# Feed-forward stage of a hybrid decoder block: norm 2 of tokens 0 to 511 before the rest, with the first products between, and half of the low parts on VectorE

## The reference, cut to what matters

```python
x = x + merged @ w_out[l]
h2 = rms_norm(x, norm2_g[l])
x = x + (jax.nn.silu(h2 @ w_ffn_gate[l]) * (h2 @ w_ffn_up[l])) @ w_ffn_down[l]
```

## Time and profile before

| what | value |
|---|---|
| median of 3 runs | 2294.84 us (2293.65 to 2296.45) |
| the profiled execution, its own time | 2295.39 us |
| span in the profile, first to last instruction | 2293.4 us |
| PE busy | 2131.7 us, 93% |
| DVE, ACT, POOL busy | 1287.4, 757.0, 921.2 us |
| norm 2 begins (first transfer of its gain) | 1587.13 us |
| first product of the first chunk | 1625.60 us |
| last product of the first chunk ends, first down matmul | 1667.97 us |
| mean granted TensorE clock | 0.967 |

### The profile page before, as it was taken

How to read it: one execution, slowest core, us unless ns; L and a number is a source line. 1 busy time by engine, 2 the same in 40 slices (tenths; PEclk the granted TensorE clock), 3 DMA queues, 4 the chain that set the end, 5 groups by cost and what they waited for, 6 DMA issues and landing times. The chain is left out here.

```text
span 2293.4 us, 29780 instructions
## 1 busy us (share of the span) xinstructions
PE 2131.7 (93%) x10088; PEld 1724.4 (75%) x10088; DVE 1287.4 (56%) x1744; ACT 757.0 (33%) x1326; POOL 921.2 (40%) x733
## 2 busy tenths in 40 slices
PE   4999989998999999999999699997799999999999
PEld 3787777777877777777877478886688888888887
DVE  4557676852275675675676466557544444444444
ACT  3223232321154454454454420002422222223322
POOL 3322222222244344344344233332855555555552
PEclk7999999999899999999999799998799999999999
DMA  3211111222414314314324172221111111111111
GB/s 104 48 34 46 28 46 30 49 48 78 99 29 101 78 41 101 78 41 101 78 41 110 70 270 74 91 83 46 56 56 44 37 47 55 55 55 55 55 55 73
DMA packets 137775, 153.84 MB, mean 67 GB/s; under 512 B 7664, under 2 KB 112112, under 8 KB 137728
## 3 DMA queue, kind: packets, MB, share of 16 engines
q1 hardware_dynamic: 136000, 150.07, 23.8%
q10 hardware_dynamic: 1728, 3.15, 0.4%
HBM read 107.06 MB, written 20.97 MB: 56 GB/s over the span
## 5 line engine op out<-in xcount | busy, mean ns | idle before, releaser
L123 POOL TENSOR_TENSOR w_hi<-w_raw,w_ones 128x64 fp32r<-128x64 f32 x88 | 34.2, 389 | 763.7 <-PE gla_g L147 362.2
L478 POOL TENSOR_TENSOR sb_rows<-sb_beta,sb_rest 128x128 f32<-128x128 f32 (+7 forms) x128 | 166.1, 1302 | 250.8 <-DVE sb_rest L833 250.8
L833 DVE TENSOR_TENSOR_SCAN sb_rest<-sb_rest 128x128 f32<-128x128 f32 (+7 forms) x128 | 205.6, 1614 | 33.6 <-ACT sb_beta L684 33.6
L126 POOL TENSOR_TENSOR w_lo<-w_raw,w_hi 128x1024 fp32r<-128x1024 f32 x88 | 218.5, 2483 | 7.3
L839 DVE TENSOR_TENSOR sb_wt_lo<-sb_t,sb_wt_hi 128x512 fp32r<-128x512 f32 x192 | 106.4, 554 | 172.3 <-ACT sb_wt_hi L692 170.3
L692 ACT CAST sb_wt_hi<-sb_t 128x512 fp32r<-128x512 f32 x192 | 92.6, 482 | 234.0 <-PE sb_t L577 232.8
L147 PE MATMUL sb_g<-h_hi,w_hi 128*128 128x512 f32 x544 | 161.1, 421 | 3.7 <-DVEq L737 3.7
L147 PE MATMUL sb_g<-h_lo,w_hi 128*128 128x512 f32 x544 | 156.3, 413 | 0.0
L147 PE MATMUL sb_g<-h_hi,w_lo 128*128 128x512 f32 x544 | 153.1, 406 | 0.0
L147 PE MATMUL gla_g<-h_hi,w_hi 128*128 128x512 f32 x480 | 132.1, 408 | 1.8 <-DVEq L1251 1.8
L577 PE MATMUL sb_t<-ident,sb_rows 128*128 128x128 f32 x576 | 102.4, 289 | 32.1 <-DVE sb_wt_lo L839 32.0
(11 more groups left out here) (310 smaller groups left out, 5084.6 us busy)
## 6 DMA issues: line engine op xcount, KB each, us to landing
w_raw<-w_in SPq DMA_DIRECT2D x64, 512.0 KB, 8.1
ff_raw_g<-w_ffn_gate SPq DMA_DIRECT2D x11, 1024.0 KB, 5.4
ff_raw_u<-w_ffn_up SPq DMA_DIRECT2D x11, 1024.0 KB, 5.8
ff_raw_d<-w_ffn_down SPq DMA_DIRECT2D x11, 1024.0 KB, 4.9
sb_qs<-sb_q_st SPq DMA_DIRECT2D x32, 256.0 KB, 5.1
sb_kh<-sb_k_st SPq DMA_DIRECT2D x32, 256.0 KB, 5.1
sb_kl<-sb_k_st SPq DMA_DIRECT2D x32, 256.0 KB, 5.0
mp_sig<-gates_t SPq DMA_DIRECT2D x16, 512.0 KB, 4.4
```

Source lines behind the costliest of these rows:

```text
L123: self.nc.gpsimd.tensor_tensor(hi[:, 0:64], raw[:, 0:64], self.ones[:], ALU.mult)
L126: self.nc.gpsimd.tensor_tensor(lo, raw, hi, ALU.subtract).then_inc(self.ready, 1)
L478: nc.gpsimd.tensor_tensor(rows[tb // 4][:, tb % 4, 0:width], beta[:, n % 2, 0:width], rest[:, n % 2, 1:width + 1], ALU.mult).then_inc(row_ ...
L833: nc.vector.tensor_tensor_scan(back, back, back, 1.0, ALU.mult, ALU.bypass).then_inc(scanned, 1)
```

## The change

The transposes and high and low parts of tiles 0 to 3 (tokens 0 to 511) are done first, and they fill all eight banks. P1 g, P1 u, P2 g and P2 u of the first chunk then run one at a time, each followed by the transposes of one pair. A pair now needs its late tile (i+4) scaled into a new buffer `xg_late`, and transposes both tiles again into banks 2, 3, 6 and 7. `xg_late` has two places and lies where the weights' ring places 4 and 5 are, so these two are filled only after the last pair's transposes (`third_product`). VectorE takes over the low parts of P5 and P7 of each pair from GpSimd. In every chunk the third product is now P5 and the fourth P3. GpSimd's list of the first chunk is written out anew.

```diff
+    ORDER = (P1, P2, P5, P3, P6, P7, P4)
...
+                def first_gate_up(norm):
+                    low(0, G, P1, 1)
+                    sums_1(G, 0)
+                    low(1, U, P1, 2)
+                    for m in (G, U):
+                        low(2 + m, m, P2, 3 + m)
+                    norm(0)
+                    sums_1(U, 0)
+                    norm(1)
+                    norm(2)
+                    for m in (G, U):
+                        low(4 + m, m, P5, 5 + m)
+                    norm(3)
+                    for m in (G, U):
+                        sum_2(m, 0, 0)
+                    for m in (G, U):
+                        sum_4(m, 0, 0)
...
-                    for n, op in enumerate((P5, P7, P6, P4)):
+                    for n, op in ((2, P6), (3, P4)):
                         pool.wait_ge(t_high, 4 * pair + n + 1)
...
+                def third_product():
+                    act.wait_ge(pair_done, 4 * PP)
+                    for n in (4, 5):
+                        high(n, n, 0)
+
+                for pair in range(PP - 1):
+                    pair_high(pair)
+                pair_high(PP - 1, third_product)
...
+                    tt(h[P3][1][:, :, cols], b22, h[P3][0][:, :, cols], ALU.subtract).then_inc(b_low, 1)
+                    for n, (op, t) in enumerate(((P5, t1), (P7, t3))):
+                        dve.wait_ge(t_high, 4 * pair + n + 1)
+                        tt(h[op][1][:, :, cols], t, h[op][0][:, :, cols], ALU.subtract).then_inc(t_low_dve, 1)
...
+                for i in range(PP):
+                    first_low(i, 0)
+                scale(PP)
+                for i in range(PP):
+                    first_low(i, 1)
                 for pair in range(PP):
+                    combine(pair)
+                    if pair + 1 < PP:
+                        scale(PP + pair + 1)
...
+                def transposes(pair):
+                    pe.wait_ge(xg_ready, PP + pair + 1)
+                    pe.wait_ge(b_low, 2 * PP + pair)
+                    need(pe, t_made, 4 * pair)
+                    late = xg_late[:, pair % 2, :]
+                    for bank, src, k0 in ((2, late, 0), (3, xg[:, pair, :], 0), (6, late, KH), (7, xg[:, pair, :], KH)):
+                        flip(bank, src, k0).then_inc(pair_done, 1)
...
                             multiply(slot(2 * n + m), bank, p)
+                            if norm and p in (P1, P2):
+                                transposes(2 * n + m)
```

More of the change, by code:

```diff
@@ L1798, in gate_up @@
                                 sum_4(m, ch, at)
+                def first_gate_up(norm):
[15 more added lines that the diff above has]
+                        sum_4(m, 0, 0)
+                    for n, p in enumerate(ORDER):
+                        if n >= 3:
+                            for m in (G, U):
+                                low((2 * n + m) % RING, m, p, 2 * n + m + 1)
                 def down_low(ch):
@@ L1893, in gate_up @@
                             y_round(3, ch)
[L1895 to L1900, removed]
-                    high(n, n, 0)
+                for i in range(PP):
+                    first_high(i)
+                    if i == 2:
+                        high(0, 0, 0)
+                for n in range(1, 4):
+                    high(n, n, 0)
+                def third_product():
[5 more added lines that the diff above has]
+                pair_high(PP - 1, third_product)
                 gate_up(0, lambda n: n % RING)
@@ L1943, in low @@
[L1943 to L1951, removed]
+                    dve.wait_ge(b12_kept, pair + 1)
@@ L2044, in _, with flip @@
             def _(pe):
+                def flip(bank, src, k0):
+                    for q in range(KH):
+                        ins = nc.tensor.transpose(tr[bank][:, q, :], src[:, (k0 + q) * P:(k0 + q + 1) * P], c["ident"][:])
+                    return ins
                 def transposes(pair):
[L2046 to L2054, removed]
+                    pe.wait_ge(xg_ready, PP + pair + 1)
[4 more added lines that the diff above has]
+                        flip(bank, src, k0).then_inc(pair_done, 1)
                 def multiply(slot, bank, op):
@@ L2103, in down_block @@
                         ins.then_inc(d_done, 1)
-                for pair in range(PP):
-                    transposes(pair)
+                for i in range(PP):
+                    pe.wait_ge(xg_ready, i + 1)
+                    for half in range(2):
+                        flip(2 * i + half, xg[:, i, :], half * KH).then_inc(tr_done, 1)
                 gate_up(0, lambda n: n % RING, 0, norm=True)
```

117 lines of the change are left out of this document (61 added, 56 removed).

## The result

The changed kernel takes 2298.71 us (median of 14 runs, 2294.60 to 2302.52) against 2293.22 for the kernel before (14 runs, 2287.39 to 2297.09): a ratio of 1.0024, 95% interval [1.0014, 1.0034]. It is slower by about 5.5 us. The profiled execution took 2301.57 us, span 2299.7, which is 6.3 more than before's 2293.4.

The account below looks back on a forecast made before the run. TensorE, busy 93% of the span, bounds the kernel; the start and length of its last unbroken run of products decide. 2295.39 + 4.3 = 2299.7, or 2299.1 against the median; it said 2299.5, range 2292.5 to 2306.

Parts of the forecast that it names:

- Head: Norm 2's first 32 transposes: cost unchanged, 6.97 us; P1 g starts about 1601.2, gaining nothing; pair 0's transposes at 1604.7.
- Pairs: Loop over late tiles: pair 0 takes 10.4 us, later ones 9.2 to 10.45; pair 3's transposes start at 1633.5 to 1636.0.
- P5 g: First half-product of P5, now third product: could start at about 1639.4 to 1643.6, gaining 1.1 us or losing 3.
- P3 g: First half-product of the fourth product: waits 6.3 us for GpSimd's sums and weight low part, starts at 1648.6 to 1652.7.
- The unbroken run: TensorE's last products of the first chunk without a wait: 8 half-products, 21.8 us, ending at 1670.4 to 1674.5.
- The number: Whole kernel's time: +4.3 us gives 2299.7 for an execution like the profiled one, 2299.1 against the median; 2299.5 said.
- Other chunks: Chunks after the first, with P5 ahead of P3: TensorE has no gap to lose there, 0.
- no meeting: Rival: VectorE's new low parts meet no GpSimd operation; full-clock period 8.0, -3.6 us, 2291.5; chance 0.17.
- clock stays up: Rival: same order, TensorE's clock stays full in the loop, all pairs at 9.2 us; +1.9, 2297; chance 0.19.
- VectorE passed over: Rival: a low part on VectorE waits until GpSimd is idle, P5 starts at about 1653; +12, 2307.5; chance 0.12.

Follow-up runs that it names:

- e1_lows_gpsimd: The changed kernel with all four low parts of each pair back on GpSimd, none of these on VectorE; 2288.19 us, ratio to before 0.9976.
- e7_p5_low_first: The changed kernel with the next scaling ahead of VectorE's low parts and, in the last pair, P5's low part right behind T3; 2290.43 us, ratio 0.9992.
- e8_filled_p5: The changed kernel with the next scaling ahead of VectorE's low parts, plus 14 extra matmuls behind pair 3's transposes; 2290.84 us, ratio 0.9991.
- e9_first_filled: e7_p5_low_first with 8 extra matmuls behind pair 3's transposes, in the wait in front of P5 g; 2289.72 us, ratio to before 0.9986.

## Why the prediction was right

The direction, the place and the mechanism held. Step by step:

- *Head.* P1 g at 1600.32 (said 1601.2) and pair 0's transposes at 1603.79 (1604.7): 0.9 us sooner, since the 32 transposes took 5.62 us, not the 6.97 of the earlier trace rows; the clock had risen at 1596.9 where it rose at 1599.5 before. P1 g gained nothing by itself, as said.
- *Pairs.* Said 10.4, then 9.2 to 10.45 with a leaning to the upper end; measured 9.94, 10.25, 10.15. The two low parts were priced at 1.2 us of work and 1.7 of turns, 2.9 in all; the rows have 2.92, 2.94, 2.94 and 3.09. Pair 3 at 1634.13 lies in 1633.5 to 1636.0.
- *P5 g* at 1641.46 (1639.4 to 1643.6), and behind P5 the wait for GpSimd's weight low part, as said. GpSimd's last low part ended at 1644.22 (1642.3 to 1646.4).
- *P3 g* at 1650.57 (1648.1 to 1652.2), 0.4 behind the middle. From the end of the last low part it took 6.35 us; 6.3 was said.
- *The unbroken run.* This is the mis-sized term. Eight half-products were put at 21.8 us, all at full clock; they took 23.68 (1650.57 to 1674.25). About 1.6 of the 1.9 us more come from the clock, which fell to half for 3.5 us just behind the wait, and which the filled wait gave back; 0.3 from P3 g itself, which behind a wait takes 2.98 us also at full clock. The prediction had allowed for a low clock in P5, where it was hidden, and not in P3, where it is not; the kernel before, with a wait of 1.59 us there, gave no sign of it. With it, +6.3 in the trace in place of +4.3, which is also beyond the +1.9 to +6.0 of the sum. The forecast's own range, +2.9 to +6.5, holds it, but the prediction gives no working for that one.
- *The number.* 2299.5 was said and 2298.71 measured, and part of that nearness is luck. The sum set out from a median of 2294.84 for the kernel before, and in this measurement it has 2293.22. As a change, +4.7 was said and +5.5 measured.
- *Other chunks.* 0 was said: from the first down matmul to TensorE's end it took 622.32 us before and 622.30 after.

The rivals: *no meeting* fell by the 1.25 to 1.76 us of L1995; *clock stays up* by 0.50 at 1610.50. *VectorE passed over* did not happen to the new low parts, all eight took their turn. But it exists. In `e1_lows_gpsimd` it came back, on the same product as in the earlier trace rows:

```profile
1643.67 4.82 DVE L2002 TENSOR_TENSOR ff_u<-ff_u,ff_cg 128x512 f32<-128x512 f32 x1
```

In the kernel after, the same product at 1649.93 took 1.04 us with the same GpSimd operations in front of and behind it, and in the other nine kernels 1.04 to 1.73. The two in which it was passed over are the two in which GpSimd makes all four low parts of the last pair; whether that is the reason no run shows, and it stays open. The Trainium skill ("SBUF — State Buffer", section "SBUF: two separate sides") has the shared port pair locked for a whole instruction by whichever starts first; the eight low parts agree, 1.25 to 1.76 us being one GpSimd operation's rest and their own length. The 4.82 and 5.05 us, which are the rest of one GpSimd operation and three whole ones, are not explained by such a lock alone.

What the prediction did not ask is which place in VectorE's queue the low parts had to have. It counted the turns right and named the scaling behind them as what waits. That P5's and P7's low parts are read only by the products behind the last pair, and in the loop only free a place of `t_tmp` for the next pair, while the scaling has a reader at once, was there to be read in the code, and was worth 10.8 us of distance.

## What to carry to other kernels

Moving work to a less busy engine pays by what waits behind it there, not by the engines' shares: VectorE had room (56% busy) and still lost, because the moved operations stood in front of the one that TensorE waited for. Put what starts the next stage first in a queue, then the work without a reader. When a gate is moved forward, price the next gate as well: in three kernels here (`e7_p5_low_first`, `e8_filled_p5`, `e9_first_filled`) what was won before or under P5 went into the wait in front of P3 g. A wait on TensorE costs more than its length where the clock falls behind it, which happened behind one of four waits of 1.6 to 2.2 us here, so count the matmuls behind a new wait at both levels.

## What was not expected of the hardware

A wait of 1.89 us, the only one in the 6.80 us at full clock from 1644.60 to 1651.40 (TensorE was busy for the other 4.91), was followed by 3.5 us at half clock (1.2 GHz). The fall came 0.8 us after TensorE had gone on, and TensorE was busy through all of these 3.5 us. With the wait filled the clock stayed at the full level, but it also stayed there behind unfilled waits of 1.59, 1.69 and 2.15 us in three other kernels. In `e8_filled_p5` a wait of 5.1 us filled for 3.4 of it did not keep the clock up but moved the fall to later. A product on VectorE between GpSimd's weight low parts took 1.04 to 1.73 us in ten kernels and 4.82 and 5.05 us in two.
